# Residual rows stored early, the last stage added onto them by accumulating transfers; routing waits and end order changed

## The reference

```python
u = _rmsnorm(x, n_pre1) * (1.0 + sc1[:, None]) + sh1[:, None]
m, buf, h_last, s_last = _mixer(u, ...)
x = x + g1[:, None] * _rmsnorm(m, n_post1)
u2 = _rmsnorm(x, n_pre2) * (1.0 + sc2[:, None]) + sh2[:, None]
f = _moe(u2, w_rg, b_rg, w_re, b_re, w_g, w_u, w_d)
x = x + g2[:, None] * _rmsnorm(f, n_post2)
return x, buf, h_last, s_last
```

## Time and profile before

| | us |
|---|---|
| median of 3 runs (592.9 to 600.13) | 595.18 |
| profiled execution | 595.51 |
| span of the profiled execution, first to last instruction | 593.6 |
| PE busy | 558.9 (94%) |
| DVE, ACT, POOL busy | 213.0, 167.3, 110.1 |
| chain that ended last: share of PE | 87% |
| chain: share of DMA, DVE, ACT | 4%, 4%, 3% |

### The profile page before, as it was taken

One profiled execution on the slowest core, in us unless ns is written; L12 is line 12 of the kernel. 1 busy time (PEld: TensorE's weight loads), 2 busy tenths in 40 slices (PEclk: granted clock), 3 DMA queues, 4 the chain that ended last, 5 costly groups with the idle time before them and its releaser, 6 DMA issues.

```text
span 593.6 us, 6528 instructions
## 1 busy us (share of the span) xinstructions
PE 558.9 (94%) x2454; PEld 337.2 (57%) x2454; DVE 213.0 (36%) x510; ACT 167.3 (28%) x325; POOL 110.1 (19%) x142
## 2 busy tenths in 40 slices
PE   2899999999999999999999998789999999999974
PEld 1567755544454544674444433567777777777631
DVE  2615266522133233343434635423222212211146
ACT  5422496612123211321323332021111111111132
POOL 4106000129000000012100103313322323231200
PEclk9999999999999999999999997899999999999998
DMA  8999747889600000099300357589999999999364
GB/s 297 387 362 346 237 189 314 310 323 294 266 1 0 1 0 0 2 356 300 107 35 1 106 203 257 166 257 344 348 338 330 356 347 327 343 353 338 59 195 160
DMA packets 69555, 132.94 MB, mean 224 GB/s; under 512 B 4526, under 2 KB 41814, under 8 KB 67474
## 3 DMA queue, kind: packets, MB, share of 16 engines
q1 hardware_dynamic: 54576, 99.36, 47.8%
q0 software_dynamic: 9968, 28.56, 17.6%
q10 hardware_dynamic: 4978, 4.58, 2.2%
HBM read 117.28 MB, written 18.35 MB: 228 GB/s over the span
## 4 chain that ended last, share of the span: by engine, by line
PE 87%; DMA 4%; DVE 4%; ACT 3%; issue 1%; ACTq 0%; SPq 0%; DVEq 0%; POOLq 0%
PE psum L689 82%; PE psum L692 6%; DMA f_dram<-arena,add_tok 2%; ACT arena L1297 1%; DMA arena<-f_dram 1%; DMA hy<-in_c_sample_dram 1%; ACT L1297 1%; DVE arena L2071 0%; ACT ss L1297 0%; DVE arena L1970 0%; DVE arena L1715 0%; DVE arena L2150 0%; DVE arena L1982 0%; DVE arena L2098 0%; DVE x L1975 0%
## 5 line engine op out<-in xcount | busy, mean ns | idle before, releaser
L689 PE MATMUL psum<-ring,arena 128*128 128x256 f32 (+1 forms) x640 | 171.9, 424 | 1.8 <-DVE arena L2150 1.3
L689 PEld LDWEIGHTS psum<-ring,arena 128*128 128x128 f32 x640 | 119.1, 190 | 38.3 <-issue 25.8
L689 PE MATMUL psum<-ring,uT 128*128 128x512 f32 (+1 forms) x384 | 126.8, 522 | 0.0
L1297 ACT ACTIVATE arena<-psum 128x512 f32<-128x512 f32 (+8 forms) x111 | 52.1, 490 | 239.0 <-PE psum L689 218.6
L689 PEld LDWEIGHTS psum<-ring,uT 128*128 128x128 f32 (+1 forms) x384 | 56.5, 172 | 60.5 <-issue 56.2
L689 PE MATMUL psum<-uT,ring 128*128 128x288 f32 x256 | 65.6, 416 | 1.2 <-ACT uT L1297 1.2
L689 PEld LDWEIGHTS psum<-uT,ring 128*128 128x128 f32 x256 | 49.2, 194 | 18.0 <-issue 4.7
L692 PEld LDWEIGHTS psum<-con,arena 128*128 128x128 f32 (+1 forms) x299 | 37.0, 149 | 26.4 <-issue 16.2
L692 PE MATMUL psum<-con,arena 128*128 128x128 f32 (+1 forms) x299 | 43.8, 286 | 6.5 <-DVE arena L1684 2.7
L1297 ACT ACT_TABLE_LOAD x33 | 42.3, 1283 | 11.3 <-PE psum L689 7.5
L2194 DVE TENSOR_TENSOR arena<-arena,psum 128x256 f32<-128x256 f32 x16 | 6.7, 421 | 94.1 <-ACT arena L1297 94.1
(11 more groups left out here) (203 smaller groups left out, 431.0 us busy)
## 6 DMA issues: line engine op xcount, KB each, us to landing
ring<-in_w_mod_dram SPq DMA_DIRECT2D x24, 1024.0 KB, 13.6
ring<-in_w_exp_gate_dram SPq DMA_DIRECT2D x16, 1024.0 KB, 15.5
ring<-in_w_exp_up_dram SPq DMA_DIRECT2D x16, 1024.0 KB, 16.2
ring<-in_w_exp_down_dram SPq DMA_DIRECT2D x16, 1024.0 KB, 12.1
ring<-in_w_in_dram SPq DMA_DIRECT2D x12, 1024.0 KB, 10.7
ring<-in_w_out_dram SPq DMA_DIRECT2D x4, 1024.0 KB, 7.2
f_dram<-in_consts_dram POOLq DMA_DIRECT2D x1, 3072.0 KB, 15.9
arena<-in_state_ret_dram POOLq DMA_DIRECT2D x6, 512.0 KB, 5.6
```

The source lines that it names most:

```text
L689: return nc.tensor.matmul(out, lhsT, rhs, start=first, stop=last)
L1297: return nc.scalar.activation(out, src, func, **kw).then_inc(done, 1)
```

## The change

What it does, part by part:

1. Output. ACT stores the residual `x` of tile t to the output right after it has issued the store of `u2` (five more transfers, `s_yout`). `finish` ends with the scaled row in `Y`; its third operation, the addition onto `x`, is gone. POOL issues five accumulating transfers that add `Y[t]` onto the output in DRAM; SP's five stores are gone. POOL ends after they have landed.
2. Order of the end. `END_ORDER = (0, 1, 4, 2, 3)` for SP's loads, PE, ACT, DVE and POOL. Tile 4 joins `ON_DVE`: DVE adds its `Y`, and PE has only the `pT` matmuls of it.
3. Function tables of ACT. A Silu on one column after the Exps and a Sqrt on one column after the last `take_out` bring the table loads forward.
4. Routing. `state_step(2)` and `(3)` move from ahead of the rank count and from ahead of the branch to between the branch and `slot_tokens(1)` and `(2)`. `keep_running` uses 128 columns instead of 512; its counts are 2, 2, 2 instead of 1, 1, 2. The five gate-weight operations of DVE (`gate_weights`) move from ahead of the rank count to behind `numbers(2)`.

The core of the diff (the slow path of the branch is changed in the same way and left out):

```diff
-ON_DVE = (0, 1)
+ON_DVE = (0, 1, 4)
+END_ORDER = (0, 1, 4, 2, 3)
...
 sp:
-                for t in range(TILES):
+                for t in END_ORDER:
                     sp.dma_start(Y[0:rows(t), t], f_dram[t * P:t * P + rows(t), :])\
                         .then_inc(s_fl[t], 16)
-            for t in range(TILES):
-                sp.wait_ge(s_fin, t + 1)
-                ...
-                sp.dma_start(dst, x[0:rows(t), t, :]).then_inc(s_yout, 16)
-            sp.wait_ge(s_yout, 16 * TILES)
...
 pool:
-            pool.wait_ge(s_store, 16 * 5)
+            pool.wait_ge(s_yout, 16 * TILES)
+            for nth_end, t in enumerate(END_ORDER):
+                pool.wait_ge(s_fin, nth_end + 1)
+                pool.dma_start(result(t), Y[0:rows(t), t], accum_op=ALU.add).then_inc(s_store, 16)
+            pool.wait_ge(s_store, 16 * (5 + TILES))
             pool.wait_ge(s_ssto, 16 * NH)
...
 pe:
-                    mm(bank[3], ident, con[:, C_COS:C_COS + 512], True, True)
+                    mm(bank[3][:, 0:P], ident, con[:, C_COS:C_COS + P], True, True)
...
             add_state(1)
-            state_step(2)
-            keep_running(1)
+            keep_running(2)
...
             last.then_inc(s_rank, 1)
-            keep_running(1)
+            keep_running(2)
...
             slot_tokens(0)
-
-            state_step(3)
...
                 for e in range(1, AHEAD):
+                    state_step(e + 1)
                     slot_tokens(e)
...
-                for t in range(TILES):
+                for t in END_ORDER:
                     add_last(t)
...
 act:
                     .then_inc(s_u2st[t % 2], 16)
+                act.dma_start(result(t), x[0:rows(t), t]).then_inc(s_yout, 16)
...
             f(gx[:, :, 4:5], gx[:, :, 4:5], ACT.Exp, s_gexp)
+            f(softp[:, 0, 0:1], eps[:, 0:1], ACT.Silu, s_act)
...
                 take_out(NE - 1)
-
-                for t in range(TILES):
+                f(softp[:, 0, 0:1], eps[:, 0:1], ACT.Sqrt, s_act)
+
+                for i, t in enumerate(END_ORDER):
...
 dve, finish:
                 v.scalar_tensor_tensor(
                     out=Y[0:n, t], in0=src[0:n], scalar=ss[0:n, 3, t, 0:1],
-                    in1=tab["g2" + tag(t)][0:n], op0=ALU.mult, op1=ALU.mult).then_inc(s_fnorm, 1)
-                dve.wait_ge(s_fnorm, 2 * t + 2)
-                v.tensor_tensor(out=x[0:n, t], in0=x[0:n, t], in1=Y[0:n, t], op=ALU.add)\
-                    .then_inc(s_fin, 1)
+                    in1=tab["g2" + tag(t)][0:n], op0=ALU.mult, op1=ALU.mult).then_inc(s_fin, 1)
...
 dve, end:
-                for t in ON_DVE:
-                    add_rest(t)
-                for t in range(TILES):
-                    finish(t, Y[:, t] if t in ON_DVE else summed[t])
+                add_rest(0, 0)
+                add_rest(1, 1)
+                for i, t in enumerate(END_ORDER):
+                    finish(i, t, Y[:, t] if t in ON_DVE else summed[t])
+                    if i == 0:
+                        add_rest(2, TILES - 1)
```

More of the change, by code:

```diff
@@ L463, in fits, with result @@
             return eng.value_load(over[0:1, 0:1], min_val=0, max_val=1) < 1
+        def result(t):
+            return (y_prompt[0, t * P:(t + 1) * P, :] if t < TILES - 1
+                    else y_sample.rearrange("b t d -> (b t) d"))
         @block.sync
@@ L1262, in _ @@
                 expert_out(NE - 1)
-                for t in range(TILES):
+                for t in END_ORDER:
                     add_last(t)
             with pe.Else():
+                for h in range(2, NH):
+                    state_step(h)
                 wg = ring[:, 0, :].rearrange("p (k n) -> p k n", n=FE)
@@ L2047, in _, with gate_weights @@
             v.tensor_tensor(out=gx[:, :, 4], in0=rm2, in1=rm1, op=ALU.subtract).then_inc(s_gin, 1)
-            dve.wait_ge(s_gexp, 2)
-            link(v.tensor_reduce(out=rtop, in_=gx[:, :, 0:NG], axis=AX.X, op=ALU.add))
-            link(v.tensor_scalar(rtmp, gx[:, :, 4], 1.0, None, ALU.add))
-            tt(rtmp, rtmp, rtop, ALU.mult)
-            link(v.reciprocal(rm1, rtmp))
-            v.tensor_tensor(out=rm2, in0=gx[:, :, 4], in1=rm1, op=ALU.mult).then_inc(s_gw, 1)
+            def gate_weights():
+                dve.wait_ge(s_gexp, 2)
+                link(v.tensor_reduce(out=rtop, in_=gx[:, :, 0:NG], axis=AX.X, op=ALU.add))
+                link(v.tensor_scalar(rtmp, gx[:, :, 4], 1.0, None, ALU.add))
+                tt(rtmp, rtmp, rtop, ALU.mult)
+                link(v.reciprocal(rm1, rtmp))
+                v.tensor_tensor(out=rm2, in0=gx[:, :, 4], in1=rm1, op=ALU.mult).then_inc(s_gw, 1)
             for k in range(2):
@@ L2142, in _ @@
                 dve.engine_nop().then_inc(s_f, TILES)
-                for t in range(TILES):
-                    finish(t, Y[:, t])
+                for i, t in enumerate(END_ORDER):
+                    finish(i, t, Y[:, t])
+            count[0] = linked
             with dve.Else():
@@ L2210, in _, with add_rest @@
                 take_out(NE - 1)
-                def add_rest(t):
-                    dve.wait_ge(s_comb, t + 1)
+                def add_rest(i, t):
+                    n = rows(t)
+                    dve.wait_ge(s_comb, i + 1)
                     dve.wait_ge(s_fl[t], 16)
-                    v.tensor_tensor(out=Y[:, t], in0=summed[t], in1=Y[:, t], op=ALU.add)\
+                    v.tensor_tensor(out=Y[0:n, t], in0=summed[t][0:n], in1=Y[0:n, t], op=ALU.add)\
                         .then_inc(s_f, 1)
-                for t in ON_DVE:
-                    add_rest(t)
-                for t in range(TILES):
-                    finish(t, Y[:, t] if t in ON_DVE else summed[t])
+                add_rest(0, 0)
+                add_rest(1, 1)
+                for i, t in enumerate(END_ORDER):
+                    finish(i, t, Y[:, t] if t in ON_DVE else summed[t])
+                    if i == 0:
+                        add_rest(2, TILES - 1)
 _INS = ['x_prompt', 'x_sample', 'state_conv', 'state_lru', 'state_ret', 'c_prompt', 'c_sample',
```

32 lines of the change are left out of this document (16 added, 16 removed).

## The result

The changed kernel takes 604.22 us (median of 4 runs, 603.03 to 609.49) where the kernel before takes 597.65 on the same chip (4 runs, 592.9 to 605.13). The ratio is 1.0158, with a 95% interval of 1.0093 to 1.0224: slower, by 1.6%. The forecast was 594.0, with a range of 589.5 to 598.5.

What follows compares the result with a forecast made beforehand. PE, 87% of the last chain, was taken to bound the kernel, leaving its waits in routing and end. Routing -0.55, table -0.4, end -1.0 and POOL's closing +0.5 gave -1.45: span 592.15, 594.0 us with 1.9 around it, range 589.5 to 598.5.

Steps and rivals of the forecast that it cites:

- Part 1, routing: Routing up to the first expert: rank count earlier, expert 0 starts 0.75 us earlier, less 0.2 for early stores, so -0.55.
- My upper bound of +0.3: Routing: with 3.6 us for both state steps, expert 0 would start at 379.6, 0.3 later than before.
- Part 2, early stores: Five more issues on ACT, about 0.4 us each, hidden except 0.2 (between 0 and 0.5) ahead of the last copy.
- Part 3, tables: First expert: the 1.28 us Silu table load leaves the chain, a wait for state stores replaces it; gain 0.4.
- Part 4, PE's end: Last stage: tile 2's load lands at 576.0, PE ends at 583.0 instead of 586.07, last DVE operation 4.3 us earlier.
- Part 4, the last transfer: End of kernel: the last accumulating transfer takes 6.2 us from POOL's issue to landing and sets the end, not the queue.
- Rival C: Output: accumulating transfers don't overlap, each starts moving only when the one before has landed; 607.1 us, chance 0.06.
- Part 4, POOL's closing: After the last landing: 0.3 us for closing plus 0.5 added for POOL, the latter between 0 and 2.
- The sign of being wrong: End of kernel: a long stretch on POOL after the last landing, named as the sign of Rival B.
- Rival B: Whole kernel: state steps slow, no table gain, accumulation queue and POOL's closing add 1.2 + 2; +3.7, 599.2 us, chance 0.12.
- A: Routing: PE keeps 2.4 GHz or regains it at once, hiding the state steps; 2.6 us more gain, 591.5, chance 0.16.
- D: Whole kernel: no effect beyond noise, stores and additions change places, routing gains go into the slow clock; 595.5 us, chance 0.16.

Runs made afterwards that it cites:

- e1: The changed kernel with the old way of output: no early stores, the addition back in finish, SP storing x; 594.77 us against 595.6, ratio 1.0014.
- e2: The kernel before with only the new output (early residual stores, five accumulating POOL transfers), tiles in order 0 to 4; 600.43 us against 595.6, ratio 1.0107.
- e4: The changed kernel with the routing edits taken back (state steps, fillers, gate weights as before); 603.52 us against 595.6, ratio 1.0176.
- e10: The changed kernel with SP's loads in the order 0, 1, 2, 4, 3, PE's order kept; one run, 603.54 us.
- e7: The changed kernel with 512-column fillers, one ahead of the rank count and two behind it; 600.17 us against 599.71, ratio 1.004.
- e9: The changed kernel with plain output stored by SP, no early stores, and 512-column fillers around the rank count; 592.83 us against 596.2, ratio 0.9937.
- e6: The kernel before with one wait added: POOL also waits for SP's five last stores; 605.69 us against 599.71, ratio 1.0109.
- e11: The kernel before once more, with no line that runs changed; one run, 596.91 us.
- e3: The kernel before with its five last stores issued plain by POOL instead of SP; 602.69 us against 595.6, ratio 1.0155.
- e8: The changed kernel with plain output, state_step(2) right behind the rank count and state_step(3) ahead of the branch; 593.02 us against 599.71, ratio 0.9976.
- e5: The changed kernel with SP instead of POOL waiting for the accumulating transfers to land; 601.38 us against 599.71, ratio 1.007.

## Why the prediction was wrong, point by point

The parts here are numbered as in the prediction.

- **Part 1, routing: forecast -0.55, measured +1.34.** Most steps came as forecast: the rank count right behind `sel`, PE's branch 0.91 (I took 1.1), `state_step(2)` 3.75 at half clock (3.6). The step that failed was `state_step(3)` and what follows it: I took 2.5, "after a stretch of dense work", and it took 3.77. The clock did not come back, though PE was busy without a pause for those 8 us. From there all of PE's steps were slow too: fillers and `turn_input(0)` took until 380.1, so PE and not DVE was the longer branch (forecast 3.0 from `slot_tokens(2)` to the expert, measured 381.00 - 377.33 = 3.67). The rest is the early store: its issue delayed ACT's copy, which starts 1.17 after A instead of 0.72, so 0.45, the upper end of my 0 to 0.5. e1, which has the same routing without the early stores, takes 23.20 from A to B, 0.47 less, and e2, the old routing with them, 0.56 more. My upper bound of +0.3 put both state steps at half clock and `turn_input(0)` behind them at full clock (1.04; it took 1.92); that was the error of thought. (In the working, `numbers(2)` starts at 374.06 and not at 373.90; its length of 0.5 is right.)
- **Part 2, early stores:** else hidden, as forecast. The fifteen experts take the same 178.6.
- **Part 3, tables: -0.4 forecast, -0.15 measured.** The mechanism was right. The Silu has no load of its own any more and waits for the state stores instead. How much is gained depends on when they land: in e4 the first expert takes 9.48, 0.74 less than before, in e10 9.94.

```profile
382.06 1.58 ACTq L1549 DMA_DIRECT2D out_dram<-arena  x2
389.38 0.87 ACT L1300 ACTIVATE arena<-psum 128x256 f32<-128x256 f32 x2 [8.63 <-DMA out_dram<-arena]
```

- **Part 4, PE's end: 3.1 forecast, 1.5 measured.** The step that failed is the landing of tile 2's load, put at 576.0 on the old axis, 7.9 after S; it came after 9.3. I counted the half tile ahead of it by its bytes, which e10 and the other profiles contradict. PE's two tiles behind it took 7.1 (forecast 7.0), and the last DVE operation came 2.7 earlier instead of 4.3.
- **Part 4, the last transfer:** 0.3 + 6.7 = 7.0 after the last DVE operation, forecast 6.3. The row was the right one to go by. Rival C is out: the third accumulation was issued at 582.77, when the first, issued at 578.78, was still under way (5.4 to its landing), and still the later ones took 6.1 to 6.8 each. The Trainium skill, DMA: Bandwidth & Descriptors, "Two DMAs through the same engine are not ordered", says that descriptors of one queue of one DMA engine start in order and are pipelined: the trace agrees in that the transfers overlap.

```profile
out_dram<-arena POOLq DMA_DIRECT2D x4, 512.0 KB, 6.6
out_dram<-arena POOLq DMA_DIRECT2D x1, 256.0 KB, 6.1
```

- **Part 4, POOL's closing: 0.3 + 0.5 forecast, "between 0 and 2", measured 6.08.** This is the step of the prediction that failed most, 5.3 of the 10.15 us by which the sum was off: POOL was taken to close in 0.8 us behind the last landing and takes 6.08, in which its DRAIN runs alone. The bound had nothing under it: no view showed POOL closing, because it had long been done. Without the 5.7 the median would have been about 598.5, at the upper edge of the range, and still not faster than the 597.65 of the kernel before in the same comparison; the forecast had started from 595.18. The sign of being wrong that I had named for this, a long stretch on POOL's side after the last landing, came.
- **The rivals.** Rival B named the right pieces (both steps slow, the queue, the closing) and stopped at 599.2, because the closing was capped at 2. Nothing in A came true, and D's "no effect" holds only for the parts without the output (e1).

By the sums: 0.4 at the start, 1.9 in routing, 0.25 in the table, 1.6 at the end of DVE, 0.7 in the landing and 5.3 in the closing, together 10.15 more than forecast: from -1.45 to +8.7. The closing is the largest; without its 5.3 the others would still have made +3.4 in this pair of profiles.

**What stays open.** What POOL's DRAIN does is not shown, only its length and that it is exposed when POOL is last. Whether it would be as long in a kernel whose POOL never issued a transfer was not run. Why the clock falls in one execution and holds in the next, with the same PE instructions (e7 and e9; the kernel before, e6 and e11), was not found; so the worth of the routing order is known only within about a us. The start moves with the clock too: A lies at 354.1 to 354.5 in the four profiles without a low clock between 20 and 35 us (e1, e3, e7, e9), at 356.0 to 358.1 in the seven with 3.4 us of it, and at 357.9 and 358.7 in the two with 6.8 (e8, e11).

## What to carry to other kernels

Before work is moved to GpSimd at the end of a kernel, ask which engine ends last: an engine that was idle has a closing that does not show in the critical chain of before, and here it cost 5.7 us, one per cent, where the whole new end was forecast to gain 0.5. Where it must be so, let another engine wait for the last transfer, so that the closing runs beside it. And a step put into PE's idle time is only hidden as long as the clock holds: price everything behind it, fillers too, at both levels.

## What the hardware showed unexpectedly

- From the last landing to the end of the span 0.40 us pass when SP waits for it, and 5.9 to 6.1 when POOL does, whether or not POOL issued the transfer (e2, e3, e6). If POOL is through with its last issue and SP waits, 3.3 (e5). POOL's DRAIN is 5.46 to 5.66 us when everything has landed before it starts, and 8.75 to 9.40 when it starts beside its last transfer, ending 2.9 behind that landing in the kernel before and 3.1 in e5.
- The last accumulating transfer from POOL takes 4.4 us for 256 KB (e2) and 6.1 to 7.3 for 512 KB (the changed kernel, e4, e5, e7, e10), a plain one 2.8 for 256 KB and 2.9 for 512 KB (e3). With others in flight the same 512 KB took up to 8.2 (e2). The indirect one of the experts took 6.2.
- In the middle of SP's five loads one of 64 rows and 256 KB costs those behind it as much as one of 128 rows and 512 KB: as third load the half tile landed 6.1 to 8.1 us after the first issue (seven profiles), a full one 6.3 to 7.9 (six), and the full load in fourth place landed 8.5 to 9.5 after the first issue behind the one and 8.9 to 9.4 behind the other. In last place it is cheaper: the half tile landed 0.5 to 0.9 behind its predecessor, a full one 1.0 to 1.3.
- The granted clock over the same PE instructions differs between executions: over the 22.2 to 26.3 us of routing 0.54 in e6, 0.77 in e11. In the changed kernel 3.75 + 3.77 us of state steps in which PE was always busy did not bring 2.4 GHz back, nor did the 3 us behind them. And 3.4 us at the low clock under dense expert matmuls cost 1.7 us (e7).
